# Feed-forward down products: one 512-column product for the high part of the weights in place of two of 256

## The reference, cut to what matters

```
D_FF = 2816
h2 = rms_norm(x, norm2_g[layer])
x = x + (jax.nn.silu(h2 @ w_ffn_gate[layer]) * (h2 @ w_ffn_up[layer])) @ w_ffn_down[layer]
```

## Time and profile before

| | |
|---|---|
| median of 3 runs | 2178.73 us (2178.36 to 2179.11) |
| profiled execution, device time | 2178.25 us |
| its span, first to last instruction | 2176.4 us |
| mean granted TensorE clock | 0.956 |
| PE busy | 1900.0 us, 87% |
| DVE busy | 774.2 us, 36% |
| ACT busy | 523.0 us, 24% |
| down products of layer 0 on PE | about 568 to 632.5 us |
| down products of layer 1 on PE | about 1212 to 1279 us |

### The profile page before, as it was taken

How to read it: one execution, slowest core, us unless ns; L and a number is a source line. 1 busy time by engine, 2 the same in 40 slices (tenths; PEclk the granted TensorE clock), 3 DMA queues, 4 the chain that set the end, 5 groups by cost and what they waited for, 6 DMA issues and landing times.

```text
span 2176.4 us, 26092 instructions
## 1 busy us (share of the span) xinstructions
PE 1900.0 (87%) x11262; PEld 1436.0 (66%) x11262; DVE 774.2 (36%) x1312; ACT 523.0 (24%) x780; POOL 0.2 (0%) x4
## 2 busy tenths in 40 slices
PE   6999999999998999998999999998999875555555
PEld 5898876799997898766799998546788421111101
DVE  3432332556533533234355665323444200000001
ACT  2201121244432011211344463423432210000000
POOL 0000000000000000000000000000000000000000
PEclk9999999999999999999999999999999998888888
DMA  6232342465432223353745442211126899999997
GB/s 260 87 114 81 117 155 97 160 193 190 175 121 92 97 97 116 155 194 136 241 155 174 157 130 64 97 39 39 39 78 248 351 409 409 409 409 409 409 409 301
DMA packets 170323, 414.13 MB, mean 190 GB/s; under 512 B 4832, under 2 KB 61408, under 8 KB 166752
## 3 DMA queue, kind: packets, MB, share of 16 engines
q1 hardware_dynamic: 169488, 408.69, 50.7%
q10 hardware_dynamic: 720, 3.78, 0.4%
HBM read 411.41 MB, written 1.05 MB: 190 GB/s over the span
## 4 chain that ended last, share of the span: by engine, by line
PE 61%; DMA 20%; DVE 11%; ACT 7%; issue 1%; SPq 0%; ACTq 0%; DVEq 0%
PE ps L219 45%; PE ps L767 7%; DMA ring<-in_w_e_down_dram 5%; ACT rarena L213 4%; DMA high<-in_w_e_up_dram 4%; DVE rarena L178 4%; DMA high<-in_w_e_down_dram 3%; PE ps L1157 3%; PE ps L1519 2%; DMA high<-in_w_e_gate_dram 2%; DMA ring<-in_w_e_gate_dram 2%; DVE low L178 2%; DVE high L178 2%; ACT high L213 1%; DMA ring<-in_w_e_up_dram 1%
## 5 line engine op out<-in xcount | busy, mean ns | idle before, releaser
L219 PE MATMUL ps<-high,ring 128*128 128x256 f32 (+1 forms) x2016 | 483.5, 391 | 7.8 <-DMA ring<-in_w_in_dram 5.9
L219 PE MATMUL ps<-rarena 128*128 128x256 f32 (+1 forms) x3648 | 460.0, 288 | 9.6 <-DVE rarena L178 7.4
L219 PEld LDWEIGHTS ps<-rarena 128*128 128x128 f32 x3648 | 448.3, 192 | 19.6 <-DVE rarena L178 10.4
L219 PEld LDWEIGHTS ps<-high,ring 128*128 128x128 f32 x2016 | 376.2, 192 | 81.5 <-issue 19.9
L213 ACT ACTIVATE high<-ps 128x512 f32<-128x512 f32 (+2 forms) x210 | 103.1, 491 | 719.9 <-PE ps L1519 286.8
L1519 PE MATMUL ps<-high,low 128*32 128x512 f32 x1040 | 161.0, 749 | 113.3 <-DMA high<-in_w_e_down_dram 38.6
L178 DVE TENSOR_TENSOR rarena<-ring,rarena 128x2048 fp32r<-128x2048 f32 x76 | 167.3, 2201 | 137.5 <-ACT rarena L213 135.9
L1519 PEld LDWEIGHTS ps<-high,low 128*32 128x32 f32 x1040 | 31.2, 126 | 228.5 <-issue 58.9
L213 ACT ACTIVATE rarena<-ring 128x2048 fp32r<-128x2048 f32 x76 | 139.9, 1841 | 156.6 <-DMA ring<-in_w_ffn_up_dram 92.3
L178 DVE TENSOR_TENSOR high<-high,ps 128x512 f32<-128x512 f32 x52 | 35.7, 687 | 323.9 <-PE ps L1519 266.0
L767 PE MATMUL ps<-high 128*128 128x128 f32 (+6 forms) x1024 | 128.9, 298 | 15.3 <-DVE high L178 10.7
(11 more groups left out here) (147 smaller groups left out, 1349.5 us busy)
## 6 DMA issues: line engine op xcount, KB each, us to landing
ring<-in_w_in_dram SPq DMA_DIRECT2D x34, 2048.0 KB, 7.9
high<-in_w_e_gate_dram SPq DMA_DIRECT2D x22, 2048.0 KB, 24.0
high<-in_w_e_up_dram SPq DMA_DIRECT2D x22, 2048.0 KB, 23.9
high<-in_w_e_down_dram SPq DMA_DIRECT2D x21, 2048.0 KB, 24.0
ring<-in_w_mod_dram SPq DMA_DIRECT2D x12, 2048.0 KB, 8.7
ring<-in_w_ffn_gate_dram SPq DMA_DIRECT2D x22, 1024.0 KB, 5.4
ring<-in_w_ffn_up_dram SPq DMA_DIRECT2D x22, 1024.0 KB, 8.0
ring<-in_w_e_down_dram SPq DMA_DIRECT2D x11, 2048.0 KB, 24.3
```

What stands on the lines that cost most here:

```text
L219: ins = self.e.matmul(out, l, r, start=first and i == 0, stop=end and i == n - 1)
```

## The change

The high and the low part of the activation become the two halves of one buffer, `F.ac`, at the same addresses. For each k tile and bank, wh is now multiplied with both halves at once, 512 columns wide, into the two halves of the bank. The third product, wl by the high part, still goes to columns 0 to 255. So a triple becomes two instructions and two loads of weights, with the same 768 columns. At the last k tile the narrow product goes first, so that the wide one ends the group. The DVE then adds both halves of a bank to x, with two additions, the second waiting for the first.

```
-        F.ach, F.acl = ralloc(22, 256), ralloc(22, 256)
+        F.ac = ralloc(2, 22, 256)
+        F.ach, F.acl = F.ac[:, 0], F.ac[:, 1]
...
-                                ins = PE.group3(bs[i][:, 0:256],
-                                                [(wh[:, k, 128 * i:128 * i + 128], wl[:, k, 128 * i:128 * i + 128],
-                                                  F.ach[:, k0 + k, :], F.acl[:, k0 + k, :])],
-                                                k0 + k == 0, k0 + k == 21)
+
+                                wi = slice(128 * i, 128 * i + 128)
+                                end = k0 + k == 21
+                                if end:
+                                    PE.e.matmul(bs[i][:, 0:256], fr(wl[:, k, wi]), fr(F.ach[:, k0 + k, :]), start=False,
+                                                stop=False)
+                                ins = PE.e.matmul(v2(bs[i]), fr(wh[:, k, wi]), fr(F.ac[:, :, k0 + k, :]),
+                                                  start=k0 + k == 0, stop=end)
+                                if not end:
+                                    ins = PE.e.matmul(bs[i][:, 0:256], fr(wl[:, k, wi]), fr(F.ach[:, k0 + k, :]),
+                                                      start=False, stop=False)
...
-                            V.tt(xi, xi, ps(f"{l}dn{half}{i}.ps")[:, 0:256], add).then_inc(*V(f"{l}x{4 * half + i}"))
+                            V.tt(xi, xi, ps(f"{l}dn{half}{i}.ps")[:, 0:256], add).then_inc(*V())
+                            V.tt(xi, xi, ps(f"{l}dn{half}{i}.ps")[:, 256:512], add).then_inc(*V(f"{l}x{4 * half + i}"))
```

## The result

The kernel after takes 2180.99 us in the median (22 runs, 2174.04 to 2191.09), the kernel before on the same chip 2176.61 us (22 runs, 2170.0 to 2180.83). The ratio is 1.0028, interval 1.0018 to 1.0038: slower by some 4 to 8 us. (It is not the ratio of the two medians, which is 1.0020; the two means lie 0.28% apart.) The single number came out (2181.0 was forecast), but that was luck: the kernel before ran 2.1 us faster here than in the three runs that the forecast started from, so the difference, 4.4 us by the medians and 6.1 by the ratio, is two to two and a half times the +2.35 us of my sum. The ratio passes the 0.2% that I had set as a bound, on the side to which I gave 15%, though its interval begins at 0.18%. The profiled execution took 2187.18 us, 6 us more than the median (span 2185.4, mean clock 0.953).

What follows compares the result with a forecast made beforehand. PE's own rate was taken as the bound (busy 87%). Layer 0's -0.60 and layer 1's +2.95 made +2.35 on 2178.25 us, so 2180.6, plus 0.48 for the median, said as 2181.0; range 2177.2 to 2184.2.

Steps and rivals of the forecast that it cites:

- my sum: Whole kernel: -0.60 us in layer 0 and +2.95 in layer 1, together +2.35 us slower.
- The pair of products: PE's down products: a triple falls from 0.3606 to 0.3471 us, saving 0.0135 each, 1.94 us per layer.
- A: From layer 0's first down product to layer 1's first unit: 64.98 us before; layer 0 forecast at -0.60.
- The gain of jobs 22 and 23: The two jobs end before existing waits in both layers, so the gain of 4 x 16 triples is lost.
- End of layer 0: Layer 1's first PE unit waits for bank ps7, which the last DVE adds free later: +1.34 us.
- Layer 1: Late low parts make jobs 30, 31, 32 wait (2.0, 0.45, 0.45 us), z1 waits 2.0: +2.95 us in all.
- B: From layer 1's context-squares sum to the z1 sum: 61.18 us before; layer 1 forecast at +2.95.
- The clock: Rival: granted clock falls to 0.50 in a new PE wait, 1.7 us per stretch (2182.7; two 2184.4); 14%.
- My last sign of being wrong: Account is wrong if the clock differs between the two profiles before 1300 us; no size given.
- The cover holds: Rival: in layer 1's first half the adds slip into idle time; -0.5 in all, 2178.2 us; 17%.
- The alternation eats the gain: Rival: alternating wide and narrow products on PE costs what was saved, jobs stay 5.77 us; +4.8, 2183.5; 7%.
- All gain is kept: Rival: no add is felt and the full 4.75 us gain arrives, 2174.0 us; 4%.

Runs made afterwards that it cites:

- moved adds: Kernel after with first-half adds placed one per job at m = 28 to 31, layer 1's last adds ahead of a low part: 2175.20 us, ratio 1.0014.
- bank 5: Kernel after with the bank ring restarted each layer, so layer 1's first unit writes the fifth-numbered bank, not ps7: 2181.93 us, ratio 1.0021.
- the wait filled: Kernel after with 14 overwritten products on PE before the z1 sum: 2178.75 us, ratio 1.0018; repeated, 2178.42 us, 1.0008.
- The adds alone: Kernel before, its three 256-column products kept, with two dependent additions per bank: 2181.45 us, ratio 1.0027 to the kernel before.
- the second time: Kernel after, unchanged, timed again beside the kernel before: 2184.33 us against 2175.36, ratio 1.0036 (1.0024 to 1.0049).
- one add: Kernel after without its second addition, x getting only columns 0 to 255 of each bank: 2176.28 us, ratio 0.9995 to the kernel before.

## Why the prediction came out as it did

**What bounds, and which waits.** Right, and this is the part that was not luck. All five places named (the first unit of layer 1, jobs 30, 31 and 32, the z1 sum) show their wait in the profile, and each of them goes when its cause is taken away: all with the second add, those of layer 1 with the moved adds, that of layer 0 with bank 5.

**The pair of products: the term that was mis-sized.** I took 0.0135 us per triple. In A, from job 24's start (578.51) to the end of the last product (628.88 + 0.23 = 629.11) are 50.60 us, against 432 x 0.1202 = 51.93 before: 1.33 us over 144 triples, 0.0092 each, and 1.33 us where I had 1.94. The wide product was priced by the earlier trace rows, 0.2269, and costs 0.2325 in four of a row. In the kernel after, two cadences turn up. These rows are the first wide products of jobs 26, 27, 31 and 32; 16 pairs lie between the first and the second, and between the third and the fourth:
```profile
589.71 0.39 PE L1141 MATMUL ps<-rarena 128*128 128x512 f32 x1
...
595.26 0.39 PE L1141 MATMUL ps<-rarena 128*128 128x512 f32 x1
...
615.01 0.40 PE L1141 MATMUL ps<-rarena 128*128 128x512 f32 x1
...
620.66 0.40 PE L1141 MATMUL ps<-rarena 128*128 128x512 f32 x1
```
Job 26 takes 5.55 us, 0.347 a pair, just what I had forecast; job 31 takes 5.65, 0.353 a pair, which is the 0.2325 and 0.1200 of four in a row. In layer 0 of this profile only jobs 25 and 26 have the quick cadence, jobs 28 to 32 the slow one. In layer 0 of all nine profiles with wide and narrow in turn, jobs 28 to 32 take 5.64 to 5.66 us; jobs 25 and 26 take 5.55 in four of them and 5.65 in five. This changes between executions of the same kernel (A of the kernel after is 64.97 in one profile and 65.3 in the other), and what picks the cadence stays open. My doubt that the alternation could cost something was right. My reason for taking the sum all the same, that both neighbours keep their pitch "to a nanosecond or so", was not: the first five wide products of the row that I had read miss it by 0.005 us. Whether the turn from narrow to wide is what costs isn't settled either, since no run has long rows of wide products in these jobs.

**The gain of jobs 22 and 23.** Lost, as said: the wait at 580.41 grew from 0.52 to 0.72 us, and the 12.33 us from the first down product to job 24 are 12.34.

**End of layer 0.** The wait is there as forecast, though the profile doesn't name the DVE as its releaser: +1.34 forecast, 1.86 - 0.56 = +1.30 measured. With 1.33 gained, A is even (-0.60 forecast).

**Layer 1.** Counted from the context-squares sum, job 30 starts 1256.45 - 1220.29 = 36.16 in, and 1258.8 - 1223.7 = 35.1 before: +1.1 (+0.8 forecast, and a wait of 1.40 in place of 2.0, as PE came later with its smaller gain). The down products end 1277.03 - 1220.29 = 56.74 in, 55.3 before: +1.4 (+0.95 forecast). The z1 sum starts +3.26 later (+2.95). So A and B make +3.25 against my +2.35; the 0.9 that lack are nearly all the pair of products (0.6 in layer 0, some 0.2 in the jobs that run free in layer 1).

**The clock.** Put at 14% as a rival, it is part of the likeliest case. The four profiles that have the z1 wait of 1.8 us behind wide products all show 0.50 over the sum; the two with the wait filled and the seven without a wait don't. The adds alone, with 1.69 us, don't either, nor do the six waits of 1.86 us at the end of layer 0. The wait of 1.97 us of the earlier trace rows is in every profile, and in the second one of the kernel before the clock stays at 1.00 behind it:
```profile
654.10:660.00 5.90, 5.90 (x26) 4.69 (x27) 1.74 (x5) 1.96 (x4) 0.00 (x0) 1.00 0.27 103
```
So a fall is not certain for a wait of this length, and the length alone doesn't decide. +3.25 and 1.7 make +4.9, and the later share of a fall, 1.8 us in the one pair of profiles that can be laid together, makes +6.7; measured were 3.9 to 8.3 (the interval of the ratio), and 5.2 to 10.7 the second time. My last sign of being wrong, a clock that differs between the two profiles before 1300 us, came up too; it was a poor sign, since the two profiles of the kernel before differ there as well. The first profile of the kernel after has one fall more that I can't put down to the change alone. The rows are the products behind the attention, before and after:
```profile
1498.00:1503.00 5.00, 5.00 (x12) 1.53 (x11) 0.00 (x0) 0.00 (x0) 0.00 (x0) 1.00 0.00 0
```
```profile
1498.00:1503.00 5.00, 5.00 (x6) 1.30 (x6) 0.00 (x0) 0.00 (x0) 0.00 (x0) 0.50 0.00 0
```
That stretch lasted 17.1 us from 1497.0, half of it lost: the same work starts 1.6 us later than in the kernel before ahead of it (1488.60 against 1487.04) and 9.7 us later behind it (1516.13 against 1506.42). So 8.15 of the 9.0 us by which the two profiled spans differ are this one stretch, and those spans must not be read as the price of the change. It is in two of the four profiles of kernels with the wait and in none of the others.

**The other rivals.** *The cover holds* fell with the wait at 1256.45. *The alternation eats the gain* fell with its price: about a third was eaten, not all. *All gain is kept* fell with the row at 631.14; the kernel with one add, which comes nearest to it, was 0.9995 (0.9983 to 1.0007).

## What to carry to other kernels

Fewer instructions on the busiest engine are a gain only where that engine's next wait doesn't end on the work they push to another: here A and B were 2.7 us shorter by it where no new wait ate the gain (1.33 and 1.37), while 16 adds of 0.46 us, 12 of them in front of results for which TensorE waits, cost A and B 4.9 us (kernel after against one add) and the clock's answer on top. Before such a trade, look where the added work stands in its engine's program. The same adds one per job, in gaps of the hand-over, cost nothing in layer 1. And a new wait of some 2 us on TensorE should be priced with the clock that may fall behind it: if the wait can't be removed, products of no use can fill it, as they did here at no cost in B. A price read from a long row of like instructions should be read from the row's beginning too.

## What the runs showed that I had not expected

- The price of a wide product in fp32r is no constant: 0.232 us for the first five of a row behind narrow ones, 0.2265 to 0.2269 after them, 0.2325 in four of a row. A wide and a narrow one in turn take 0.347 or 0.353 us, with one cadence held through a job.
- Work that only fills PE's wait (14 products, 1.84 us) kept the granted clock at 1.00 and took the median from 2184.33 to 2178.42 us on one chip, 5.9 us, though the sum itself gives back only 1.7. The first timings of the same two kernels, on two chips, lie only 0.1% apart in their ratios.
- Executions of one kernel differ in how long the clock stands at 0.50 (44.2 and 64.6 us before 1720 us in two profiles of the kernel before), and their spans by 7.6 us. A change of 2 us in A or B is plain in the stretch and can't be read in the median.
